# Latent attention of a fused transformer kernel: turning the next pair's queries ahead, half an output step behind the turned probabilities, scores ahead of the weighing

## What is computed

```
kv, q_lat   = parts of rmsnorm(x) @ mla_w_in            # latent rows, 256 and 128 wide
q, k, v     = up-projections; q and k are 64 wide plus 32 rotated, normed over 96
o_mix       = softmax(causal(q k^T)) v                  # 12 heads, 256 rows
o_mem       = softmax(q_mem k_mem^T) v_mem              # 4 heads over 256 memory rows
x           = x + concat(o_mix, o_mem) @ w_out          # 1024 x 1024
x           = x + conv_ffn(rmsnorm(x))
```

## Time and profile before

| what | us |
|---|---|
| median of 3 runs | 1300.1 (1298.56 to 1300.38) |
| the profiled execution, its own time | 1298.19 |
| its span, first to last instruction | 1296.8 |
| PE busy in the span | 1280.0 |
| attention loop of the latent layer, PE from the turned probabilities of pair 2 to the weighing of pair 7 | 1056.89 to 1101.02 |

### The profile page before, as it was taken

How to read it: one execution, slowest core, us unless ns; L and a number is a source line. 1 busy time by engine, 2 the same in 40 slices (tenths; PEclk the granted TensorE clock), 3 DMA queues, 4 the chain that set the end, 5 groups by cost and what they waited for, 6 DMA issues and landing times.

```text
span 1296.8 us, 19918 instructions
## 1 busy us (share of the span) xinstructions
PE 1280.0 (99%) x7878; PEld 1119.0 (86%) x7878; DVE 971.3 (75%) x1545; ACT 693.7 (53%) x1019; POOL 152.8 (12%) x237
## 2 busy tenths in 40 slices
PE   8999999999999999999999999999999989999999
PEld 8988999889998898888888878888888867888887
DVE  6457477978656747766667777798888887888888
ACT  5345566545535556643334755655554775655553
POOL 8000001000000000200001231000000160000000
DMA  9531445433734635566665633366665612466662
GB/s 321 179 129 68 165 163 199 163 98 119 244 142 160 211 117 179 154 189 194 194 195 164 203 129 107 90 204 195 189 188 179 222 34 82 127 206 188 187 203 81
DMA packets 209468, 212.72 MB, mean 164 GB/s; under 512 B 7969, under 2 KB 156595, under 8 KB 209376
## 3 DMA queue, kind: packets, MB, share of 16 engines
q1 hardware_dynamic: 205632, 206.25, 50.4%
q0 software_dynamic: 3152, 4.15, 1.0%
q10 hardware_dynamic: 592, 1.05, 0.2%
HBM read 210.25 MB, written 1.05 MB: 163 GB/s over the span
## 4 chain that ended last, share of the span: by engine, by line
PE 90%; DVE 4%; ACT 3%; issue 2%; POOL 1%; DMA 0%; ACTq 0%; DVEq 0%; POOLq 0%
PE psum_b L2254 9%; PE psum_a L2254 9%; PE psum_a L538 6%; PE psum_a L540 6%; PE psum_a L539 6%; PE psum_b L538 6%; PE psum_b L540 6%; PE psum_b L539 6%; PE psum_c L538 5%; PE psum_b L2257 5%; PE psum_c L539 5%; PE psum_a L2257 5%; PE psum_c L540 5%; DVE w_lo L487 1%; PE psum_c L1706 1%
## 5 line engine op out<-in xcount | busy, mean ns | idle before, releaser
L477 ACT ACTIVATE w_hi<-raw 128x2048 fp32r<-128x2048 f32 (+3 forms) x231 | 368.2, 1631 | 24.3 <-PE psum_b L540 12.9
L487 DVE TENSOR_TENSOR w_lo<-raw,w_hi 128x2048 fp32r<-128x2048 f32 (+3 forms) x154 | 338.8, 2216 | 43.9 <-ACT w_hi L477 41.1
L2254 PE MATMUL psum_b<-x,w_hi 128*128 128x512 f32 x528 | 165.6, 395 | 0.0
L2254 PE MATMUL psum_a<-x,w_hi 128*128 128x512 f32 x522 | 164.1, 396 | 0.0
L2257 PEld LDWEIGHTS psum_b<-x,w_lo 128*128 128x128 f32 x528 | 99.2, 188 | 23.2
L500 DVE TENSOR_TENSOR w_lo<-raw,w_hi 128x512 fp32r<-128x512 f32 (+1 forms) x159 | 116.2, 734 | 2.6 <-ACT w_hi L477 2.6
L2257 PEld LDWEIGHTS psum_a<-x,w_lo 128*128 128x128 f32 x522 | 98.1, 188 | 22.8
L2410 ACT ACTIVATE ffn_pre<-ffn_both,cols 128x256 f32<-128x256 f32 x88 | 50.3, 602 | 113.0 <-DVE ffn_both L2422 113.0
L2454 POOL CAST ffn_hidden_hi<-ffn_h 128x256 fp32r<-128x256 f32 x66 | 51.2, 775 | 485.1 <-DVE ffn_h L2441 330.2
L538 PE MATMUL psum_c<-w_hi,ffn_hidden_hi 128*128 128x512 f32 x264 | 103.6, 392 | 0.6 <-DVE ffn_hidden_lo L2446 0.5
L2257 PE MATMUL psum_b<-x,w_lo 128*128 128x256 f32 x528 | 103.7, 278 | 0.0
(11 more groups left out here) (583 smaller groups left out, 2990.3 us busy)
## 6 DMA issues: line engine op xcount, KB each, us to landing
raw<-in_ffn_w_up_dram SPq DMA_DIRECT2D x88, 512.0 KB, 5.0
raw<-in_w_in_dram SPq DMA_DIRECT2D x39, 1024.0 KB, 5.5
raw<-in_w_gu_dram SPq DMA_DIRECT2D x44, 512.0 KB, 5.2
raw<-in_ffn_w_down_dram SPq DMA_DIRECT2D x44, 512.0 KB, 3.5
raw<-in_w_down_dram SPq DMA_DIRECT2D x22, 512.0 KB, 3.4
raw<-in_w_br_ssm_dram SPq DMA_DIRECT2D x8, 1024.0 KB, 5.1
raw<-in_w_xkv_dram SPq DMA_DIRECT2D x8, 1024.0 KB, 5.8
raw<-in_w_out_dram SPq DMA_DIRECT2D x8, 1024.0 KB, 5.7
```

What stands on the lines that cost most here:

```text
L477: act.activation(k.w_hi[:, s, 0:size], k.raw[:, s, 0:size], ACT.Copy).then_inc(*k.rounded.at(*key))
L487: dve.tensor_tensor(k.w_lo[:, s, 0:size], k.raw[:, s, 0:size], k.w_hi[:, s, 0:size].bitcast(F32), ALU.subtract).then_inc(*k.split.at(*key))
L2254: pe.matmul(ps[:, 512 * j:512 * j + 512].rearrange("p (n t) -> p n t", n=2), hi[j], k.X_both[:, :, kt, :], start=kt == 0, stop=False, skip ...
```

## The change

The diff in full:

```
--- before.py
+++ after.py
@@ -3645,6 +3645,15 @@
         pe_lat_scores(k, n + 1)
 
 
+def pe_lat_attend_early(k, n, fill):
+
+    pe_lat_turn_pair(k, n + 1)
+    pe_fox_turn_prob(k, n, LatPair)
+    take(fill, 1)
+    pe_lat_scores(k, n + 1)
+    pe_fox_weigh(k, n, LatPair)
+
+
 def pe_mla(k):
     p = mla_products(k)
     k.nc.tensor.wait_ge(*k.ffn_both.by("ffn0", FT - 2, 1))
@@ -3661,26 +3670,27 @@
     pe_lat_rope(k, 0)
     pe_lat_attend(k, 1)
     take(p, 2)
-    a, b = lat_out(k, 0, 1), lat_out(k, 1, 1)
+    a, b = lat_out(k, 0, 1, True), lat_out(k, 1, 1, True)
     take(p, 1)
-    pe_lat_attend(k, 2)
+    pe_lat_attend_early(k, 2, a)
     take(a, 1)
     pe_lat_rope(k, 1)
+    take(a, 2)
+    pe_lat_attend_early(k, 3, a)
     take(a, 1)
-    pe_lat_attend(k, 3)
-    take(a, 2)
-    take(b, 1)
-    pe_lat_attend(k, 4)
+    take(b, 3)
+    take(a, 1)
+    pe_lat_attend_early(k, 4, a)
     take(b, 1)
     pe_lat_rope(k, 2)
-    take(b, 1)
-    pe_lat_attend(k, 5)
+    take(b, 2)
+    pe_lat_attend_early(k, 5, b)
     take(b, 1)
     a, b = lat_out(k, 0, 0, True), lat_out(k, 1, 0, True)
     take(a, 2)
     take(b, 2)
-    pe_lat_attend(k, 6)
-    take(a, 2)
+    pe_lat_attend_early(k, 6, a)
+    take(a, 1)
     take(b, 2)
     take(a, 2)
     pe_fox_turn_prob(k, 7, LatPair)
@@ -3692,9 +3702,9 @@
 
 
 def act_lat_attend(k, n):
-    act_fox_turn_prob(k, n, LatPair)
     if n < PAIRS - 1:
         act_lat_turn_pair(k, n + 1)
+    act_fox_turn_prob(k, n, LatPair)
     act_fox_out(k, n, LatPair)
 
 
@@ -3728,8 +3738,8 @@
     act_split(k, 1)
     act_lat_exp(k, 2)
     act_up_queries(k, 2)
+    act_lat_turn_pair(k, 3)
     act_fox_turn_prob(k, 2, LatPair)
-    act_lat_turn_pair(k, 3)
     act_up_keys(k, 2)
     act_up_values(k, 2)
     act_fox_out(k, 2, LatPair)
@@ -3785,8 +3795,8 @@
     dve_up_keys(k, 1)
     dve_fox_normalize(k, 2, LatPair)
     dve_split_part(k, 2, 3)
+    dve_lat_turn_pair(k, 3)
     dve_fox_turn_prob(k, 2, LatPair)
-    dve_lat_turn_pair(k, 3)
     dve_split_part(k, 0, 3)
     dve_up_queries(k, 2)
     dve_up_means(k, 2)
@@ -3796,36 +3806,36 @@
     dve_fox_normalize(k, 3, LatPair)
     dve_lat_rope(k, 1)
     dve_up_keys(k, 2)
+    dve_lat_turn_pair(k, 4)
     dve_fox_turn_prob(k, 3, LatPair)
-    dve_lat_turn_pair(k, 4)
     dve_split_part(k, 1, 3)
+    dve_lat_peaks(k, 4)
     dve_fox_out(k, 3, LatPair)
     dve_split_part(k, 2, 3)
-    dve_lat_peaks(k, 4)
     dve_fox_normalize(k, 4, LatPair)
     dve_split_part(k, 0, 3)
+    dve_lat_turn_pair(k, 5)
     dve_fox_turn_prob(k, 4, LatPair)
-    dve_lat_turn_pair(k, 5)
     dve_split_part(k, 1, 3)
+    dve_lat_peaks(k, 5)
     dve_fox_out(k, 4, LatPair)
     dve_split_part(k, 2, 3)
-    dve_lat_peaks(k, 5)
     dve_fox_normalize(k, 5, LatPair)
     dve_lat_rope(k, 2)
+    dve_lat_turn_pair(k, 6)
     dve_fox_turn_prob(k, 5, LatPair)
-    dve_lat_turn_pair(k, 6)
     dve_split_part(k, 0, 3)
+    dve_lat_peaks(k, 6)
+    dve_fox_out(k, 5, LatPair)
     dve_split_part(k, 1, 3)
-    dve_fox_out(k, 5, LatPair)
     dve_split_part(k, 2, 3)
-    dve_lat_peaks(k, 6)
     dve_fox_normalize(k, 6, LatPair)
+    dve_lat_turn_pair(k, 7)
     dve_fox_turn_prob(k, 6, LatPair)
-    dve_lat_turn_pair(k, 7)
     dve_split_part(k, 0, 3)
+    dve_lat_peaks(k, 7)
     dve_fox_out(k, 6, LatPair)
     dve_split_part(k, 1, 3)
-    dve_lat_peaks(k, 7)
     dve_fox_normalize(k, 7, LatPair)
     dve_fox_turn_prob(k, 7, LatPair)
     dve_split_part(k, 2, 3)
```

## The result

The changed kernel took **1308.78 us**, the median of 6 runs (1306.99 to 1313.13), the kernel before 1299.47 beside it (6 runs, 1297.64 to 1300.38): a ratio of 1.0082, 95% interval 1.0063 to 1.0101, so slower by 0.6 to 1.0%. The forecast was 1307.7 with a range of 1303.6 to 1311.5. It stood on the 1300.1 of the earlier runs of the kernel before; beside the kernel that now ran with it the change costs 9.3 us, where 7.6 had been forecast. The six runs are of two kinds. Three, with a granted clock of 0.999 or 1.000 over the span, took 1306.99, 1307.66 and 1307.78; three with 0.993 to 0.996 took 1309.79, 1312.91 and 1313.13. The profiled execution is one of the second kind, 1309.79 (span 1308.2). So the forecast case A holds in half of the runs, and A with B's falling clock in the other half.

The account below looks back on a forecast made before the run. PE, busy 99% of the span, bounds the kernel. Loop idle was to grow from 4.3 to 11.9 us (1.85 + 6.48 + 1.34 + 0.73 + 1.32 + 0.17), 7.6 slower: 1300.1 becomes 1307.7 us, range 1303.6 to 1311.5.

Parts of the forecast that it names:

- case A: The forecast: on ACT, y_hi and the rounding queue behind a later weighing and hold the exponentials; 7.6 us slower, chance 0.72.
- Rival B: PE's clock falls as well in the two long idles, adding 3.3 us in all: 1311.0 us; chance 0.12.
- Idle before 4.3 us, all that this change can win inside the loop: PE idle in the old attention loop, pair 2's turned probabilities to pair 7's weighing: 4.3 of 44.13 us, 0.3%.
- W behind S: exponentials two us late: Weighing behind scores: exponentials of pairs 3, 4, 5 and 7 start 2.99 us after scores end, against 1.00 before.
- Idle 3.24: PE idle ahead of turned queries of pairs 4 and 6, waiting for DVE's rotated copy: 3.24 us each.
- Idle 1.34: PE idle ahead of stream b's half steps, waiting for DVE's last third of weight piece X2: 1.34 us.
- 0.73: PE idle after pair 5's weighing, waiting for DVE's thirds of weight piece X4: 0.73 us.
- 0.37 ahead of every score: PE idle between turned queries and scores, 2.14 us apart, waiting for copies: 0.37 us a step, five steps 1.85.
- Idle 1.32: PE idle at pair 7's turned probabilities, held by late exponentials: 1.32 us.
- Rival C: The stalls go: exponentials not held, weighing is pure filling, only 1.85 us idle stays; 2.4 us faster, 1297.7; chance 0.08.
- Rival D: Idle only moves: stalls overlap or waits for thirds don't count; within 2.6 us of before, about 1301; chance 0.08.
- The loads: Loads behind weight pieces X2 and X4 go out some 5 and 8.5 us later; priced at nothing.

Follow-up runs that it names:

- e_free: Changed kernel with rounding ahead of y_hi, weight thirds ahead of peaks, rotated parts behind scores, and four half steps in each of three gaps: 1297.34 us, ratio 0.9990.
- e_round: Changed kernel with ACT's rounding of a weight piece moved ahead of y_hi, nothing else: 1303.0 us, ratio 1.0032.
- e_warm12: Changed kernel with 12 calls of a filler matmul in each of PE's two long waits: 1306.81 us, ratio 1.0060.
- e_early_rope: Changed kernel with rounding ahead of y_hi, two weight thirds earlier, and rotated parts turned behind scores of pairs 3 and 5 and copied earlier: 1298.35 us, ratio 0.9995.
- e_round_thirds: Changed kernel with ACT's rounding ahead of y_hi and two thirds of weight pieces ahead of DVE's peaks: 1300.3 us, ratio 1.0011.
- e_old_bal: Kernel before, in its own order, with rotated parts turned behind the scores and copied earlier, and five half steps per gap: 1297.45 us, ratio 0.9992.
- e_warm12_thirds: Changed kernel with 12 filler calls in each long PE wait and two thirds of weight pieces ahead of DVE's peaks: 1305.68 us, ratio 1.0052.
- e_thirds: Changed kernel with two thirds of weight pieces on DVE moved ahead of the peaks of pairs 4 and 6: 1309.51 us, ratio 1.0082.
- e_late: Kernel before with only the weighing moved behind the next pair's scores on PE, from pair 2 on: 1312.62 us, ratio 1.0105.
- e_turn: Kernel before with only the next pair's turned queries ahead of the turned probabilities, from pair 2 on: 1303.3 us, ratio 1.0044.

## Why the prediction was right

**"Idle before 4.3 us, all that this change can win inside the loop."** No order won more than a quarter of it: the shortest loop of the runs is 43.14 (e_free), 1.0 under before's 44.13.

**"W behind S: exponentials two us late."** They start 5.15 behind the start of the scores; the forecast, 2.05 of scores and 2.99, was 5.04. Before it was 3.05. e_round undid this alone: 4.5 us above before where e_warm12, at the same clock, is 8.3 above, so the late exponentials cost 3.8. This is shown.

**"Idle 3.24" ahead of R4 and R6.** 1063.86 to 1066.98, which is 3.12, and 3.13 at R6. The releaser is the forecast one.

**"Idle 1.34" at b, "0.73" at X4.** In e_warm12 the steps S4 to R5 and S6 to R7 take 7.88 and 7.15; without these waits they take 6.51 (e_early_rope) and 6.47 (e_round_thirds): 1.37 and 0.68.

**"0.37 ahead of every score."** R to S took 2.17 to 2.23 at the full clock, forecast 2.14.

**"Idle 1.32" at T7.** The starts of T7's heads give about 1.2; S7 to W7 is 9.30, forecast 9.15.

**What was mis-sized.** With the clock up the walk gave a loop of 51.74 and e_warm12 measured 52.74; 8.3 to 8.6 us slower, not 7.6. The step that failed is "busy times there overlap, so I count the idle from start to start": W, S and h were priced by their distances in the old order, and in the new one other kinds of matmul meet. In the timeline of the changed kernel the weighing starts 0.43 behind the mask (1060.00 to 1060.43), where before the half step did so in 0.34 (1078.25 to 1078.59 in the earlier trace rows). The first matmul of the half step behind the weighing keeps its follower for 0.34 (1061.23 to 1061.57), where behind the scores of the kernel before it did so for 0.24 (1078.59 to 1078.83). The timeline of PE before, the mask ahead of that half step and the half step's second matmul:
```profile
1078.25 0.50 PE L3551 MATMUL psum_c<-causal_r,ident_r 128*128 128x256 f32 x2
...
1078.83 0.39 PE L539 MATMUL psum_b<-w_lo,y_hi 128*128 128x512 f32 x1
```
In sum it is 0.19 a step, and nothing of it is in the waits view. Where no wait takes it up it shows in full. In e_free S4 to R5 has scores, weighing and four half steps, by the forecast's prices 5.62, and takes 5.84:
```profile
1067.30 0.93 PE L3539 MATMUL psum_c<-mla_qk_t 64*128 64x128 f32 x8 [0.22 <-DVE mla_prob_t L2882]
...
1073.14 0.38 PE L3512 MATMUL psum_c<-ident,mla_q_nope 128*128 128x128 f32 x2
```
In e_warm12 a wait follows in every step, so the longer half step is hidden and only part of this comes through. Step by step, from the scores to the next turned queries (at the end to W7), it takes 0.10, 0.23, 0.10, 0.11 and 0.15 more than the walk, 0.69 in all. In the steps from S3, S5 and S7 some 0.1 of that is the later weighing, which starts ACT's chain. From turned queries to scores it takes 0.31 more in five steps, over half of it at pairs 3 and 4 (2.25 and 2.20 for 2.14). So about 0.3 of the 1.0 is traced to a cause, and the rest is not. The junctions may also be why e_free gains no more than e_old_bal, though its copies are better hidden.

**Rival B** was given a chance of 0.12 and came in half of the runs. The argument against it, that PE works without a pause ahead of each idle, did not hold; the argument that nothing of the like was in the trace was a reason to be less sure. Its price was too low: 3.3 was for two falls, and one fall alone cost 3.7 in the profiled execution, where the clock stayed low for 10 us and not for 4; the two slowest runs are some 5.5 above the others. The Trainium skill, "TensorE: Matmul & The Clock Gate" (HAM oscillation), warns of stretches of idle between bursts, and half of these runs agree with it. The waits here, 3.1 us, are somewhat shorter than the gaps that its rule names, so what was measured goes beyond it; the other half of the runs kept the clock.

**The median** came 1.1 above the forecast, and part of that closeness is luck. Against the kernel before the difference was 9.3, not 7.6: by e_warm12 some 0.7 of this is the queues and 1.0 the clock, which was low in half of the runs. The kernel before had run 0.6 faster than the base of the forecast, which hid a part.

**Rival C** had its price in the wrong place. "The rounding would have to be 0.9 us" was worked out for a step without rotated parts. e_round took the rounding out of the way of all of them and was still 4.5 us slower, because in pairs 3 and 5 the rotated copy follows the exponentials on ACT and R follows it (1.46 and 1.17 us of wait), and because of the thirds (e_round_thirds took off another 2.7). **Rival D** is refuted: the waits did not overlap, but for half of the thirds' (e_warm12_thirds).

**The loads** that go out later were priced at nothing; the part behind W7 took 195.8 us as before, which agrees. They were not changed alone.

**Left open:** what decides whether the clock falls in a given execution of one and the same kernel. The profiled execution kept it through the first wait of 3.1 us and lost it behind the second, that of e_thirds lost it at both.

## What to carry to other kernels

When an operation is moved later on one engine, follow the instruction that waits for it into the queue of its own engine: the cost here was not the weighing but the 1.8 us rounding and the exponentials that stood in line behind its y_hi. A long operation that depends on nothing recent belongs ahead of such a wait, not behind it; moved so, the rounding gave back 3.8 us. And before a new order is credited with hiding waits, try the same filling in the old order: here that, with the rotated parts moved, was worth as much.

## What the runs showed of the hardware

The clock of PE fell to 0.50 with waits of 3.1 us in some executions only. By the shares of the clock in the microseconds around, it fell 1.4 us after PE had started again in the changed kernel (1087.93, 0.65 in the microsecond from 1089), and in the profile of e_thirds once 0.8 after (1066.88) and once 0.6 before (1088.79). It stayed low for 10 us of unbroken work in the one, for some 3 us each in the other. The windows view of e_thirds (us, PE busy, granted clock, DMA share, GB/s):
```profile
1067.00:1068.00 1.00, 1.00 (x9) 0.85 0.00 0
1068.00:1071.00 3.00, 3.00 (x14) 0.50 0.00 0
1088.00:1089.00 1.00, 0.21 (x1) 0.59 0.00 0
1089.00:1091.00 2.00, 2.00 (x11) 0.50 0.00 0
```
The prediction had taken 4 us from the earlier trace rows. It also fell in all four runs of e_late, where no wait was over 1.1 us in the profile but several came close together, and to 0.997 over the span in one of four runs of e_turn, whose profiled execution has none over 1.2. With 2.8 us of fillers in each wait of 3.1 it fell in none of ten runs. At the start of the program the clock column does not show the level: it reads 1.00 from 3 to 7 us, though a filler takes 0.23 us there; at a clock of 0.50 two transposes of the same size take 0.42 (e_thirds, 1089.25 to 1089.67), and one takes 0.11 at 1.00.

An f32 matmul of 128 columns against the identity is two entries of 0.11 us in the trace; one that counts a filler in calls has to double it.

Where one kind of matmul follows another, 0.09 to 0.10 us can be added that no wait shows (the weighing behind the mask, the half step behind the weighing); in e_free this came to 0.2 in a step.
